# Key and query norms spread by transposed blocks, and the compressed attention branch in one step per head instead of four

## The reference, cut to what matters

```python
qn = rms_norm(q, g_q)      # per token and head, over 64 values
kn = rms_norm(k, g_k)
...
p = softmax(qn @ kn.T * scale + forget terms, causal)
```

```python
kc, vc = compress_tokens(k_c), compress_tokens(v_c)       # 31 compressed keys and values
p_c = masked_softmax(q @ kc.T * scale, c_start + 31 <= t) # branch 0, compressed
o_cmp = p_c @ vc
o_slc = ...   # branch 1, selected blocks (all of them at this length, causal)
o_win = ...   # branch 2, window of 512 (all earlier keys at this length)
out = g0 * o_cmp + g1 * o_slc + g2 * o_win
```

## Time and profile before

| what | value |
|---|---|
| median of 3 runs | 4743.85 us (4741.12 to 4752.13) |
| the profiled execution | 4743.25 us |
| its span, first to last instruction | 4741.1 us |
| mean granted TensorE clock | 0.975 |
| busy: PE, DVE, ACT, POOL | 96%, 58%, 37%, 13% |

### The profile page before, as it was taken

One profiled execution on the slowest core, in us unless ns is written; L12 is line 12 of the kernel. 1 busy time (PEld: TensorE's weight loads), 2 busy tenths in 40 slices (PEclk: granted clock), 3 DMA queues, 4 the chain that ended last, 5 costly groups with the idle time before them and its releaser, 6 DMA issues.

```text
span 4741.1 us, 62364 instructions
## 1 busy us (share of the span) xinstructions
PE 4532.1 (96%) x22235; PEld 3794.6 (80%) x22235; DVE 2748.4 (58%) x4483; ACT 1747.5 (37%) x2917; POOL 611.1 (13%) x639
## 2 busy tenths in 40 slices
PE   8999999999999999999999989899999899999998
PEld 6887788878878877888878878688666788888887
DVE  5436445454334446445454268654696867777777
ACT  3224534332232226334232233343224734444444
POOL 0000000000000000000000000000385622222221
PEclk9999999999999999999999998989999999999999
DMA  3222210122222222211222222022122588888887
GB/s 127 93 103 82 89 63 36 64 88 97 99 90 95 101 85 83 101 38 36 89 89 97 97 83 81 1 75 86 71 89 111 210 302 298 294 305 299 291 309 258
DMA packets 86660, 605.09 MB, mean 128 GB/s; under 512 B 10752, under 2 KB 11136, under 8 KB 19904
## 3 DMA queue, kind: packets, MB, share of 16 engines
q1 hardware_dynamic: 58320, 412.95, 23.9%
q0 software_dynamic: 27136, 162.28, 10.1%
q10 hardware_dynamic: 1008, 27.26, 1.4%
HBM read 573.09 MB, written 29.36 MB: 127 GB/s over the span
## 4 chain that ended last, share of the span: by engine, by line
PE 85%; DVE 6%; ACT 3%; issue 3%; DVEq 1%; DMA 1%; ACTq 1%; SPq 0%; POOL 0%; POOLq 0%
PE PB L189 24%; PE PB L191 24%; PE PB L190 24%; PE PB L2511 3%; PE PB L897 2%; PE PB L1099 2%; PE PB L2762 1%; PE PB L888 1%; PE PB L2778 1%; PE PB L2028 1%; ACT WH L2918 1%; PE PB L1112 1%; PE PB L1121 1%; DVE PT L928 1%; DVE XL L238 0%
## 5 line engine op out<-in xcount | busy, mean ns | idle before, releaser
L189 PE MATMUL PB<-XH,WH 128*128 128x512 f32 (+1 forms) x3280 | 1260.6, 384 | 60.9 <-DVE WL L170 22.5
L191 PE MATMUL PB<-XH,WL 128*128 128x512 f32 (+1 forms) x3280 | 1248.6, 381 | 0.0
L190 PE MATMUL PB<-XL,WH 128*128 128x512 f32 (+1 forms) x3280 | 1248.1, 381 | 0.0
L170 DVE TENSOR_TENSOR WL<-RAW,WH 128x1024 fp32r<-128x1024 f32 x520 | 644.7, 1278 | 507.9 <-ACT WH L162 488.9
L189 PEld LDWEIGHTS PB<-XH,WH 128*128 128x128 f32 x3280 | 624.5, 190 | 173.3 <-issue 23.6
L162 ACT ACTIVATE WH<-RAW 128x1024 fp32r<-128x1024 f32 x506 | 507.8, 1049 | 556.5 <-PE PB L191 533.3
L190 PEld LDWEIGHTS PB<-XL,WH 128*128 128x128 f32 x3280 | 624.2, 190 | 104.0 <-issue 1.4
L191 PEld LDWEIGHTS PB<-XH,WL 128*128 128x128 f32 x3280 | 623.0, 190 | 102.0
L248 POOL TENSOR_TENSOR SQ<-SQ 128x512 f32<-128x512 f32 x49 | 70.4, 1436 | 2690.4 <-ACT SQ L231 2680.5
L2968 DVE TENSOR_TENSOR WL<-RAW,WH 128x1024 fp32r<-128x1024 f32 x220 | 269.6, 1226 | 221.6 <-ACT WH L2918 219.1
L189 PE MATMUL PB<-WH,WGH 128*128 128x512 f32 x768 | 301.2, 392 | 15.5 <-DVE WGL L2984 15.5
(11 more groups left out here) (403 smaller groups left out, 7414.2 us busy)
## 6 DMA issues: line engine op xcount, KB each, us to landing
RAW<-weights SPq DMA_DIRECT2D x382, 1024.0 KB
gate_matrix<-STG ACTq DMA_DIRECT2D x6, 4096.0 KB, 12.3
GM<-gate_matrix POOLq DMA_DIRECT2D x128, 192.0 KB, 4.5
RAW<-weights SPq DMA_DIRECT2D x10, 512.0 KB, 3.9
X<-x SPq DMA_DIRECT2D x4, 512.0 KB, 5.3
x_home<-X ACTq DMA_DIRECT2D x1, 2048.0 KB, 6.8
UV<-rows,IDX POOLq DMA_INDIRECT x128, 6.2
AE<-x_home SPq DMA_DIRECT2D x1, 2048.0 KB, 14.6
```

The source lines that it names most:

```text
L170: c.nc.vector.tensor_tensor(c.WL[p][:, cols], c.RAW[p][:, cols], c.WH[p][:, cols].bitcast(F32), ALU.subtract).then_inc(c.sem("w_split"), 1)
L189: c.nc.tensor.matmul(out, wh, xh, start=start, stop=False)
L190: c.nc.tensor.matmul(out, wh, xl, start=False, stop=False)
L191: return c.nc.tensor.matmul(out, wl, xh, start=False, stop=stop)
```

## The change

There are three edits.

1. `spread` issues a transposition of each block in place of a matmul with the identity. It is still 8 for each pair.
2. The compressed branch of one head is one step over its four query blocks, with 4 x 32 scores side by side in a bank. A chunk has 18 steps: 8 selection steps, three window steps, the merged step of head 0, three window steps, the merged step of head 1, and two window steps. VectorE takes four maxima in one instruction and adds them to the scores itself (into the buffer PM); ScalarE takes the exponential in place, with no sum; VectorE sums after it has copied the turned blocks. The bank takes the mask of all four blocks first and then the four products with the keys. The turning makes four blocks of 32 rows, and the product goes to four places.
3. The work of `between` gets new step numbers. Every tap still has its place in chunks 0 and 1; one of chunk 0's ten moves from the window part to the selection part. One of the four centring instructions moves to the start of chunk 2, and two of the four reciprocals of the layer norm (L2214 before) to steps 0 and 1 of chunk 3. The SiLU follows step 8 of chunk 3 in place of step 10.

```diff
+def parts(step):
+
+    if "merged" in step:
+        return [(qb, qb * 32, 32) for qb in range(QB)]
+    return [(kb, kb * P, w) for kb, w in blocks(step["nk"])]
...
     def turn(j):
         pe.wait_ge(c.sem("p_ready"), st.count + (j + 4))
         pe.wait_ge(c.sem("pt_copied"), st.count + (j + 1))
-        for kb, w in blocks(st.steps[j]["nk"]):
+        for kb, at, w in parts(st.steps[j]):
             last = c.nc.tensor.transpose(c.PB[:w, 4 + j % 2, kb * P:kb * P + P],
-                                         st.PM[:, j % st.depth, kb * P:kb * P + w], c.IDENT[:, :])
+                                         st.PM[:, j % st.depth, at:at + w], c.IDENT[:, :])
         last.then_inc(c.sem("pt_ready"), 1)
 
     def product(j):
         step = st.steps[j]
         pe.wait_ge(c.sem("pt_copied"), st.count + (j + 3))
-        bl = blocks(step["nk"])
-        for kb, w in bl:
-            last = c.nc.tensor.matmul(step["out"], st.PT[:w, j % 2, kb * P:kb * P + P], step["values"](kb),
-                                      start=kb == 0, stop=kb == len(bl) - 1)
+        bl = parts(step)
+        merged = "merged" in step
+        for kb, _, w in bl:
+            last = c.nc.tensor.matmul(step["out"](kb) if merged else step["out"],
+                                      st.PT[:w, j % 2, kb * P:kb * P + P], step["values"](kb),
+                                      start=merged or kb == 0, stop=merged or kb == len(bl) - 1)
...
+            if "merged" in st.steps[j]:
+                S4 = c.PB[:, st.banks[m], :nk].rearrange("p (q k) -> p q k", q=QB)
+                c.nc.vector.reduce_max(c.NM4[:, m, :], S4, axis=AX.X, negate=True)
+                dve.drain()
+                c.nc.vector.tensor_tensor(st.PM[:, m, :nk].rearrange("p (q k) -> p q k", q=QB), S4,
+                                          c.NM4[:, m, :].unsqueeze(2).to_broadcast([P, QB, 32]), ALU.add)\
+                    .then_inc(c.sem("m_ready"), 1)
+                return
...
+        bl = parts(st.steps[j])
+        w = bl[0][2]
         c.nc.vector.tensor_copy(st.PT[:w, j % 2, :len(bl) * P], c.PB[:w, 4 + j % 2, :len(bl) * P])\
             .then_inc(c.sem("pt_copied"), 1)
+        if "merged" in st.steps[j]:
+            nk = st.steps[j]["nk"]
+            c.nc.vector.reduce_sum(st.steps[j]["merged"],
+                                   st.PM[:, j % st.depth, :nk].rearrange("p (q k) -> p q k", q=QB), axis=AX.X)\
+                .then_inc(c.sem("cmp_summed"), 1)
...
+        summed = sum("merged" in x for x in st.steps[:max(j - st.depth + 1, 0)])
+        if summed:
+            act.wait_ge(c.sem("cmp_summed"), summed)
+        if "merged" in step:
+            c.nc.scalar.activation(st.PM[:, m, :nk], st.PM[:, m, :nk], ACT.Exp).then_inc(c.sem("p_ready"), 1)
+            if between:
+                between(j)
+            continue
...
-                last = c.nc.tensor.matmul(c.PB[:, 6 + g, qb * P:qb * P + P],
-                                          c.RE[:, g, qb, :], c.IDENT[:, :],
-                                          start=True, stop=True)
+                last = c.nc.tensor.transpose(c.PB[:, 6 + g, qb * P:qb * P + P], c.RE[:, g, qb, :], c.IDENT[:, :])
...
 HEADS_UP_DOWN = [x for n in range(QB) for x in ((0, n), (1, QB - 1 - n))]
-CHUNK_STEPS = [(1, hh, qb) for hh, qb in HEADS_UP_DOWN] + \
-    [(br, hh, qb) for hh, qb in HEADS_UP_DOWN for br in (2, 0)]
+WINDOW_STEPS = [(2, hh, qb) for hh, qb in HEADS_UP_DOWN]
+CHUNK_STEPS = [(1, hh, qb) for hh, qb in HEADS_UP_DOWN] + WINDOW_STEPS[:3] + [(0, 0, None)] + \
+    WINDOW_STEPS[3:6] + [(0, 1, None)] + WINDOW_STEPS[6:]
...
-    return 32 if br == 0 else P * qb + P
+    return QB * 32 if br == 0 else P * qb + P
...
-            if (hh, qb) == HEADS_UP_DOWN[0] and br == 0:
-                pe.wait_ge(c.sem("qc_ready"), ch + 1)
-                pe.wait_ge(c.sem("cmp_kv"), 1)
+            if br == 0:
+                if hh == 0:
+                    pe.wait_ge(c.sem("qc_ready"), ch + 1)
+                    pe.wait_ge(c.sem("cmp_kv"), 1)
+                c.nc.tensor.matmul(SB[:, :nk], c.IDENT[:, :], c2(c, "cmask"), start=True, stop=False)
+                for q in range(QB):
+                    last = c.nc.tensor.matmul(SB[:, q * 32:q * 32 + 32], Q[:, q * P:q * P + P], K[:, g, :],
+                                              start=False, stop=q == QB - 1)
+                return last
             c.nc.tensor.matmul(SB[:, :nk], Q[:, qb * P:qb * P + P], K[:, g, :nk], start=True, stop=False)
-            if br == 0:
-                return c.nc.tensor.matmul(SB[:, :32], c.IDENT[:, :], c2(c, "cmask")[:, qb * 32:qb * 32 + 32],
-                                          start=False, stop=True)
...
-        if ch < LAST_CHUNK and j == 10:
+        if ch < LAST_CHUNK and j == 8:
...
-        if (ch, j) == (1, 16):
+        if (ch, j) == (1, 13):
...
-        if (ch, j) == (2, 16):
+        if (ch, j) == (2, 13):
...
-        if (ch, j) == (3, 10):
+        if (ch, j) == (3, 8):
...
-        if ch == 1 and 18 <= j < 18 + CC:
-            k = j - 18
+        if (ch, j) in ((1, 15), (1, 16), (1, 17), (2, 0)):
+            k = (ch * CHUNK + j) - (CHUNK + 15)
...
-        if ch == 2 and 19 <= j < 19 + 4:
-            if j == 19:
+        if (ch, j) in ((2, 16), (2, 17), (3, 0), (3, 1)):
+            k = (ch * CHUNK + j) - (2 * CHUNK + 16)
...
-TAP_STEPS = (1, 4, 6, 8, 11, 14, 17, 19, 21, 23)
+TAP_STEPS = (1, 4, 5, 6, 8, 13, 14, 15, 16, 17)
```

More of the change, by code:

```diff
@@ L1996, in nsa_nk, with nsa_merged @@
 def nsa_nk(br, qb):
-    return 32 if br == 0 else P * qb + P
+    return QB * 32 if br == 0 else P * qb + P
+def nsa_merged(c, ch, br, hh):
+    return {"merged": c.SUM2[:, ch % 2, 0, hh:8:2]} if br == 0 else {}
 def nsa_steps(c, steps):
-    sums = [(ch % 2) * 24 + br * 8 + qb * 2 + hh for ch, br, hh, qb in NSA_STEPS]
+    sums = [(ch % 2) * 24 + br * 8 + qb * 2 + hh if br else None for ch, br, hh, qb in NSA_STEPS]
     return Steps(STEPS_LAYERS, steps, (c.PM2, c.PT2, c.SUM2[:, :, :, :].rearrange("p v b e -> p (v b e)")), sums)
@@ L2038, in values, with out @@
             return c.VSW[:, kb, at:at + HD]
-        return {"nk": nk, "scores": scores, "values": values,
-                "out": c.PB[:, br, qb * P + hh * HD:qb * P + hh * HD + HD]}
+        def out(q):
+            return c.PB[:, br, q * P + hh * HD:q * P + hh * HD + HD]
+        return {"nk": nk, "scores": scores, "values": values, "out": out if br == 0 else out(qb),
+                **nsa_merged(c, ch, br, hh)}
     def between(s):
@@ L2091, in between @@
         ch, j = s // CHUNK, s % CHUNK
-        if ch < LAST_CHUNK and j == 12:
+        if ch < LAST_CHUNK and j == 11:
             act_compressed_query(c, act, ch + 1)
@@ L2095, in between @@
             act_turned(c, act, ch - 1)
-        if (ch, j) in ((1, 22), (1, 23), (2, 0), (2, 1)):
-            k = ((1, 22), (1, 23), (2, 0), (2, 1)).index((ch, j))
+        if ch == 2 and j < CC:
+            k = j
             act.wait_ge(c.sem("ln_centred"), k + 1)
@@ L2101, in between @@
                 last.then_inc(c.sem("ln_square"), 1)
[L2102 removed]
+        if (ch, j) == (2, 15):
             act.wait_ge(c.sem("ln_sum"), 2)
@@ L2110, in between @@
                 A.activation(c.YC[:, k, :], c.YC[:, k, :], ACT.Silu, bias=c.PR2[:, b:b + 1])
-        if ch == 3 and 12 <= j < 12 + CC:
-            k = j - 12
+        if ch == 3 and 9 <= j < 9 + CC:
+            k = j - 9
             if k == 0:
@@ L2115, in between @@
             A.activation(c.YH2[:, k, :], c.YC[:, k, :], ACT.Copy).then_inc(c.sem("conv2_hi"), 1)
-    act_steps(c, act, nsa_steps(c, [{"nk": nsa_nk(br, qb)} for ch, br, hh, qb in NSA_STEPS]), between)
+    act_steps(c, act, nsa_steps(c, [{"nk": nsa_nk(br, qb), **nsa_merged(c, ch, br, hh)}
+                                    for ch, br, hh, qb in NSA_STEPS]), between)
     phase_mark(c, act, cur)
@@ L2229, in dve_nsa @@
                     p2(c, "cmp_b1").unsqueeze(2).to_broadcast([P, 2, 2]), ALU.add).then_inc(c.sem("cmp_bias"), 1)
-    dve_steps(c, dve, nsa_steps(c, [{"nk": nsa_nk(br, qb)} for ch, br, hh, qb in NSA_STEPS]), between)
+    dve_steps(c, dve, nsa_steps(c, [{"nk": nsa_nk(br, qb), **nsa_merged(c, ch, br, hh)}
+                                    for ch, br, hh, qb in NSA_STEPS]), between)
     dve_branch_gain(c, dve, LAST_CHUNK, (0, 2))
```

19 lines of the change are left out of this document (9 added, 10 removed).

## The result

The changed kernel takes 4692.41 us (median of 4 runs, 4688.71 to 4695.69), the kernel before 4746.6 us in the runs beside it (4741.12 to 4752.13). The ratio is 0.9886, with a 95% interval of 0.9868 to 0.9903: 54 us faster, give or take 8. The prediction said 29 us and 4715, and its range ended at 4703. The profiled execution after took 4695.69 us, the slowest of its four, while that of before was 3.3 us under its median; its span is 47.4 us under that of before (4741.1). What follows compares these two spans unless it says otherwise.

What follows compares the result with a forecast made beforehand. TensorE was taken to bound the attention's dense stretches, and hand-overs between short instructions the mixer. Spread 14 us plus mixer 15 made 29, from 4743.85 to 4715 us; bounds 4707 to 4724, widened to 4703 to 4729.

Steps and rivals of the forecast that it cites:

- The spread's own work: Attention's spread: eight transpositions cost 0.80 us in place of 1.70, 0.90 saved in each of 16 spreads, 14 us.
- The price that the prediction set against it: Attention's spread: at the Trainium skill's 275 ns each, eight transpositions cost 2.2 us, giving +8 in place of -14.
- Clock in the attention: Attention: no term of its own, only 3 us either way for where half-clock stretches fall.
- transpositions letting the clock fall: Attention: each spread leads to about 3 us at half clock, 24 us lost against 29, 4739 us; chance 0.05.
- The merged step: Mixer: 2.3 us of TensorE time each, replacing four compressed steps; gain from hand-overs, as 96 steps become 72.
- Moved work: Mixer, starts of chunks 2 and 3: one centring and two reciprocals, about 2.6 us of work, charged -1.5.
- Behind the SiLU: Chunk 3's window part: what follows the stop, 26.9 us, was to show no change within 1 us.
- the earlier stop: Chunk 3's window part: exponentials stop for the SiLU some 1.0 us in, in place of 3.5; gain 2.5 us.
- Carried to the end: Behind the mixer: everything starts from its result, so the mixer's gain reaches the end of the kernel.
- The range: Whole kernel: spread 13 to 15, clock 3 us either way, mixer 6 to 22; together 20 to 37 us.
- the mixer's upper bound of 22: Mixer: largest gain in us, with wide steps at 1.74 us and no moved work charged.
- three signs of being wrong: Window parts of chunks 1, 2 shrink under 3 us; clock there below 0.9; spread's successor starts 1.3 us or later.

## Why the prediction was right in direction and too small

- **The spread's own work: right.** 0.91 us a spread, 16 of them, some 14.5 us. The price that the prediction set against it, 2.2 us for eight transpositions, took a duration for a distance: a record of this trace does last 0.27 us, and eight of them still take 0.79. The two figures do not contradict each other.
- **Clock in the attention: the step that failed.** The sum allowed "3 us either way for where half-clock stretches fall". The excess of the pairs fell from 17.4 us (22.1 in the second profile of before) to 8.4 (7.2): 9 to 15 us. Over all profiles here it is 12.7 to 22.1 us with 16 records (six profiles) and 4.4 to 12.3 with 8 (seven), 10 us apart in the mean. In the sum it was counted as noise, while it depends on the program. The rival that had it the other way, transpositions letting the clock fall, had the right place and the wrong sign. The Trainium skill's rule ("TensorE: Matmul & The Clock Gate", Part 4: PE-mode transpose) that transposing does not count as TensorE being busy in the same way makes no difference here: 16 records of either kind give 28.1 and 29.7 us, 8 of either kind 27.2. These are stretches of 0.8 to 1.7 us between dense matmuls; no run has a long one.
- **The merged step: right.** 2.1 us (2.3), a single compressed step 1.17 (1.3); chunk 1's window part gave 5.1 (5.8), and chunk 3's at full clock, with nothing moved, 5.1.
- **Moved work: mis-sized, and given back.** I charged 1.5 us for one centring instruction and two reciprocals; the selection parts of chunks 1 to 3 lost 5.3 together. By VectorE's timeline one tap, three centrings and three reciprocals crossed into them, 6.3 us of work, because I took VectorE's step number for the place in time. (A second tap went to chunk 0's selection part, as planned.) The window parts that they left gained by it: chunk 2's gave 7.5 us against 5.5. Another part of that is clock. In before the layer norm's second sum met the half clock and took 4.47 us; after, in the chain in order of time, it takes 0.97 less:

```profile
3032.57 3.50 PE PB L2108 x8
```

  What is left of the 2.0 is not priced by any run.
- **Behind the SiLU: the second failure.** "That is no change within 1 us" counted the records that remain at half clock and let the half clock last as long as it had. It lasted less than a third as long, 6.8 us for 23.9. The 2.5 us for the earlier stop came (2.7, to the end of the stop); behind it 27.1 us became 19.4, a gain of 7.6 where the prediction had none. It is not the chance of one execution: the part takes 25.9 us in both profiles of the changed kernel and in two other programs with its mixer, 27.4 and 27.7 in the two with 16 records in the spread, and 36.2 to 39.0 in the four profiles with the old steps and the SiLU. Taken together the part gave 10.3 us for 2.5: 5.1 by merging, measured at full clock, and 5.2 with the clock.
- **Carried to the end: right.** Behind the mixer the spans differ by 3 us more, not less.
- **The range: too narrow by its own terms.** Its 20 to 37 us is not the sum of its bounds, which is 16 to 40, so the terms were taken as if their errors did not go together. And the mixer's upper bound of 22 is more than its parts give (14.8, with wide steps at 1.74 and nothing charged, makes some 19). The measured 54 is outside all of these. None of the three signs of being wrong came: chunks 1 and 2 shrank by 5.1 and 7.5 us, their clock was 1.00 and 0.99, the spread's successor started after 0.79 us. No sign looked at the attention's clock or behind the SiLU, where the miss lies.

Together, in the first pair of profiles: 13.6 for the fifteen spreads up to the last `EXPD`, 9.0 of clock in the attention's 14 distances, less 3.2 that the other stretches up to there took more; 4.0 from there to the mixer, with the sixteenth spread's 0.9 in them; 21.0 in the mixer for 14.8, of which 5.2 are the clock behind the SiLU; and 3.0 behind it. That is 47.4, and some 30 of it (14.4 and 15.8), as much as the forecast, are the change's own work. Between the attention and the mixer most programs here take 701 to 708 us (one took 714), so what is left of that 4.0 is no term of the change.

**Open:** why the clock falls with a pair of 28.1 us and one of 27.65, and seldom with 27.2. Only the pattern is shown, by twelve programs, and it is not clean: with 8 records the excess reached 12.3 us in one program, with 16 it was 12.7 in another. In the second layer of before three of the four falls come right behind the token sums and the four transpositions after them, but the same stretch of the other pairs, and of every pair of that layer after, has none. Open too is why the kernel with 16 transpositions takes 8 us more than that with the old matmuls, though attention and mixer agree within 1 us. Their profiled executions differ by 3.2 us in span, and by 7 in the stretch between attention and mixer, whose code is the same in both.

## What to carry to other kernels

In a loop of dense TensorE work, measure the distance from one turn to the next and look for its shortest recurring value; what the others have more is clock, and it can change with the loop's length by as much as the work that was cut, in either direction. So price such an edit with the clock as a term of its own, from rows at both levels, and widen the range to the whole of the present loss (17 to 22 us here) rather than to a few us. Use a program that changes only the loop's length, as the one with 16 transpositions does, and several runs of it: one profile of the same program can differ from the next by 8 us. And merge narrow steps of a ring for their hand-overs (four steps of 1.17 us became one of 2.1), but find in the trace where each moved instruction lands on its engine, since a step's number is not its time.

## What the runs showed of the hardware

- fp32 transpositions of 128x128 between dense matmuls follow each other at 0.10 us (eight in 0.79 us) though each lasts 0.27, and a matmul of that shape is two such records (0.106 each). In stretches of 0.8 to 1.7 us the two kinds are the same for the clock.
- Twelve records in each spread took as long as sixteen (medians of 4722 us against 4720 and 4728), though their work is 7 us less, and eight took 4691 to 4692: the time at half clock does not follow the work.
- With a stop of about 4 us TensorE's clock was at half for 6.8 us in the changed kernel, for 10.2 in the program with the same mixer code and the old spread, and for 23.9 and 37.3 us in two executions of the kernel before.
